# Second attention, stage boundaries, gates and low parts of a two-block transformer kernel: slabs, turns and copies in another order

## The reference, cut to what matters

```python
# first block, twice
h = rms_norm(x, norm_w)
q, k, v, z, q_h, f_h, i_h, g_h, gate_a, gate_h = split(h @ w_in)
a = window_attention(rope(q), rope(k), v, sinks) * silu(z)
b = rms(hgrn2(silu(q_h), f_h, i_h)) * silu(g_h)
x = x + (sigmoid(gate_a) * (a @ w_up_attn) + sigmoid(gate_h) * (b @ w_up_hgrn)) @ w_out
# second block, twice; the six vectors of mod come from silu(c) @ ada_w (48 slabs of 128 rows)
h = x * (1 + sc_t) + sh_t
y = mixer(h) @ w_o              # top-k attention, then differential attention
x = layer_norm(ALPHA * x + (1 + g_t) * y)
h = x * (1 + sc_c) + sh_c
x = layer_norm(ALPHA * x + (1 + g_c) * (square(relu(h @ w1)) @ w2))
```

## Time and profile before

| | us |
|---|---|
| median of 3 runs | 1178.76 |
| lowest, highest | 1177.69, 1179.79 |
| the profiled execution | 1179.56 |
| its span | 1177.8 |
| PE, POOL busy | 1080.7, 770.3 |
| ACT, DVE busy | 550.6, 507.2 |

### The profile page before, as it was taken

How to read it: one execution, slowest core, us unless ns; L and a number is a source line. 1 busy time by engine, 2 the same in 40 slices (tenths; PEclk the granted TensorE clock), 3 DMA queues, 4 the chain that set the end, 5 groups by cost and what they waited for, 6 DMA issues and landing times.

```text
span 1177.8 us, 16431 instructions
## 1 busy us (share of the span) xinstructions
PE 1080.7 (92%) x6638; PEld 910.6 (77%) x6638; DVE 507.2 (43%) x733; ACT 550.6 (47%) x769; POOL 770.3 (65%) x379
## 2 busy tenths in 40 slices
PE   5899989997899899899898999999999798999995
PEld 5877867886678687697577998897887378988984
DVE  5765433338555323465848101106725648110015
ACT  4654565455445654444543544444445334454441
POOL 5786665766665657573045887887875147888884
PEclk9999999998999999999999999999999799999998
DMA  7647733555375435663873868765667823755640
GB/s 242 207 125 277 230 110 116 160 174 162 97 275 196 130 105 145 223 223 108 303 250 110 300 219 281 252 216 161 211 211 240 304 90 111 222 187 181 194 144 36
DMA packets 112802, 221.63 MB, mean 188 GB/s; under 512 B 14945, under 2 KB 21463, under 8 KB 112727
## 3 DMA queue, kind: packets, MB, share of 16 engines
q1 hardware_dynamic: 107552, 210.30, 54.3%
q10 hardware_dynamic: 5174, 10.28, 2.5%
HBM read 219.48 MB, written 1.07 MB: 187 GB/s over the span
## 4 chain that ended last, share of the span: by engine, by line
PE 70%; DVE 12%; ACT 7%; POOL 6%; issue 4%; ACTq 1%; DMA 1%; DVEq 0%; SPq 0%; POOLq 0%
PE lin_ps L352 12%; PE lin_ps L353 11%; PE lin_ps L354 11%; PE tmp_ps L359 5%; POOL wlo L962 5%; PE tmp_ps L360 5%; PE tmp_ps L361 5%; PE lin_ps L359 3%; PE lin_ps L360 3%; PE lin_ps L361 3%; PE tmp_ps L612 3%; ACT whi L1071 2%; PE tmp_ps L511 2%; PE tmp_ps L414 1%; DVE qst L1464 1%
## 5 line engine op out<-in xcount | busy, mean ns | idle before, releaser
L962 POOL TENSOR_TENSOR wlo<-ring,whi 128x1024 fp32r<-128x1024 f32 (+2 forms) x304 | 733.4, 2424 | 337.3 <-ACT whi L1071 329.8
L1071 ACT CAST whi<-ring 128x1024 fp32r<-128x1024 f32 (+2 forms) x304 | 313.0, 1034 | 465.6 <-PE lin_ps L354 252.4
L352 PE MATMUL lin_ps<-whi,hThi 128*128 128x512 f32 (+2 forms) x528 | 209.7, 397 | 28.6 <-POOL wlo L962 14.5
L353 PE MATMUL lin_ps<-wlo,hThi 128*128 128x512 f32 (+2 forms) x528 | 204.3, 387 | 0.0
L354 PE MATMUL lin_ps<-whi,hTlo 128*128 128x512 f32 (+2 forms) x528 | 203.8, 386 | 0.0
L359 PE MATMUL tmp_ps<-hThi,whi 128*128 128x256 f32 x520 | 148.6, 286 | 6.0 <-DVEq L1756 5.5
L352 PEld LDWEIGHTS lin_ps<-whi,hThi 128*128 128x128 f32 x528 | 101.7, 193 | 61.7 <-issue 21.6
L360 PE MATMUL tmp_ps<-hTlo,whi 128*128 128x256 f32 x520 | 147.9, 284 | 0.0
L361 PE MATMUL tmp_ps<-hThi,wlo 128*128 128x256 f32 x520 | 147.8, 284 | 0.0
L1828 DVE TENSOR_TENSOR arena<-tmp_ps,arena 128x1024 f32<-128x1024 f32 x16 | 19.6, 1225 | 229.0 <-ACT arena L1286 228.9
L354 PEld LDWEIGHTS lin_ps<-whi,hTlo 128*128 128x128 f32 x528 | 101.6, 192 | 20.1
(11 more groups left out here) (273 smaller groups left out, 1496.7 us busy)
## 6 DMA issues: line engine op xcount, KB each, us to landing
ring<-in_mlp_w SPq DMA_DIRECT2D x128, 512.0 KB, 4.4
ring<-in_ada_w SPq DMA_DIRECT2D x82, 512.0 KB, 4.8
ring<-in_w_in SPq DMA_DIRECT2D x80, 512.0 KB, 5.4
ring<-in_b_w_in SPq DMA_DIRECT2D x24, 512.0 KB, 4.5
ring<-in_w_out SPq DMA_DIRECT2D x16, 512.0 KB, 3.4
arena<-in_ada_w SPq DMA_DIRECT2D x27, 256.0 KB, 5.1
ring<-in_a_w_in SPq DMA_DIRECT2D x12, 512.0 KB, 6.8
ring<-in_w_up_hgrn SPq DMA_DIRECT2D x8, 512.0 KB, 3.4
```

The lines of the kernel that those rows point to most:

```text
L352: pe.matmul(ps, xh, hi, start=first, stop=False, skip_group_check=True)
L353: pe.matmul(ps, xh, lo, start=False, stop=False, skip_group_check=True)
L962: pool.tensor_tensor(wlo[:, n % PARTS, :, 0:width], ring[:, u % RING, 2 * h:2 * h + 2, 0:width], whi[:, n % PARTS, :, 0:width].bitcast(F32 ...
L1071: act.copy(whi[:, n % PARTS, :, 0:width], ring[:, u % RING, 2 * h:2 * h + 2, 0:width]).then_inc(S("high_formed"), 1)
```

## The change

It is a bundle of edits to the order of work. Nothing that is computed changes.

1. **Second attention.** Before, 8 slabs stood in visits of 4, 2 and 2 after turns 4, 5 and 6. Now there are four visits of 2 after turns 6, 7, 8 and 9, and the first weights of w_o are reserved after turn 6. `ada_close` moves with the first visit. The DVE reads the visits after quads 6 and 7 and around `heads_scaled(0)`.
2. **Boundaries into s0 to s3.** `mixed` goes block by block instead of by pairs, over alternating banks (`BANKED`). One or both turns go to `lin_ps` (`TURNED_IN_LIN`). In s1 and s2 tile 0 is turned before the slabs. The filler of 4 stands behind the first product's opened PSUM; s3's filler goes from 16 to 12. `project` and the MLP's end finish column half 0 of y whole before the last products of half 1, and DVE's `residual` adds half 0 of both tiles first. `affine` is spread over the first MLP groups.
3. **Gates of f0 and f1.** ACT copies the gates and z raw; Silu and Sigmoid follow after the attention, in SBUF, on ACT. The turn of `a` moves from behind the `uh` products to between halves of the second.
4. **Low parts of f0 and f1.** POOL forms each `wlo` half in two instructions.
5. **End.** Tile 0's last scaling goes over ACT and POOL, tile 1's stays in PSUM until its last step on DVE; the four outputs wait on two semaphores.

```diff
+BANKED = (0, 2, 1, 3)
+TURNED_IN_LIN = {"s0": 1, "s1": 2, "s2": 1, "s3": 2}
+BUSY = {"f0": 14, "f1": 4, "s0": 4, "s1": 0, "s2": 0, "s3": 12}
...
+                if between and not early:
+                    between()
+                ps = opened_turn(0).rearrange("p a b -> p (a b)")
+                if early:
+                    tile(ps, 0)
+                    between()
+                else:
+                    keep_busy(ps[:, 0:HALF], BUSY[name])
+                    tile(ps, 0)
+                mm = tile(ps, 1)
+                closed_turn(mm, 0)
+                ps = opened_turn(1).rearrange("p a b -> p (a b)")
...
+                def turn_a():
+                    pe.wait_ge(S("f_a"), L + 1)
+                    feature_major(f"f{L}aT", hs[:, :, 0:HALF], 4)
...
-                    linear_tok(f"f{L}uh{c}", I["w_up_hgrn"][L], c * HALF, HALF, hT, kts=4, k_src=4)
-                pe.wait_ge(S("f_a"), L + 1)
-                feature_major(f"f{L}aT", hs[:, :, 0:HALF], 4)
+                    linear_part(f"f{L}uh{c}", I["w_up_hgrn"][L], c * HALF, HALF, hT, 0, kts=4, k_src=4,
+                                mid=turn_a if c else None)
...
-                part(0, 0)
-                output_turned(name, 1)
-                part(1, 0)
-                last_by_tiles(name, [opened[f"{name}y{c}"] for c in range(2)], w, 4, hT, 4)
+                linear_part(f"{name}y0", w, 0, HALF, hT, 0, half=turn_lin[f"{name}o0"][0],
+                            mid=lambda: output_turned(name, 1))
+                linear_part(f"{name}y0", w, 0, HALF, hT, 4)
+                opened[f"{name}y1"] = open_lin(f"{name}y1", turn_lin[f"{name}o1"][0])
+                last_by_tiles(name, w, [(1, 0, hT, 0, True, ()), (1, 4, hT, 4, False, ())])
...
-            mixed("s0", lambda: [reserve(*latent(k0)) for k0 in (0, 4)])
+            mixed("s0")
...
-                      after={4: lambda: (reserve(HALF, (slice(0, HALF), win(I["b_w_o_2"][0], 0, HALF, 0))), ada(4)),
-                             5: lambda: ada(2), 6: lambda: ada(2)})
+                      after={6: lambda: (reserve(HALF, (slice(0, HALF), win(I["b_w_o_2"][0], 0, HALF, 0))), ada(2)),
+                             7: lambda: ada(2), 8: lambda: ada(2), 9: lambda: ada(2)})
...
+                    cuts = (slice(0, 1), slice(1, 2)) if n < halves_at["f1y1"][0] else (slice(0, 2),)
+                    for cut in cuts:
+                        source = ring[:, u % RING, 2 * h:2 * h + 2, 0:width]
+                        ins = pool.tensor_tensor(wlo[:, n % PARTS, cut, 0:width], source[:, cut, :],
+                                                 whi[:, n % PARTS, cut, 0:width].bitcast(F32), ALU.subtract)
...
-                    read(act.activation(dst, ps, ACT.Sigmoid), name)
+                    read(act.copy(dst, ps), name)
...
+                act.wait_ge(*read_of(f"f{L}gh1"))
+                act.activation(zs[:], zs[:], ACT.Silu).then_inc(S("f_gates"), 1)
+                for c in range(2):
+                    cols = slice(c * HALF, (c + 1) * HALF)
+                    act.activation(gh[:, :, cols], gh[:, :, cols], ACT.Sigmoid).then_inc(S("f_gates"), 1)
+                high_parts(formed[0] + 1, halves_at[f"f{L}aT0"][1])
+                for c in range(2):
+                    cols = slice(c * HALF, (c + 1) * HALF)
+                    act.activation(ga[:, :, cols], ga[:, :, cols], ACT.Sigmoid).then_inc(S("f_gates"), 1)
...
+                        if k >= 2:
+
+                            act.wait_ge(S("mixed_low"), count.get("mixed_act", 0) + kk - 1)
...
+                dve.wait_ge(*done[f"{name}y0"])
+                summed(0, 0)
+                summed(1, 0)
+                dve.wait_ge(*done[f"{name}t1"])
+                summed(0, 1)
+                statistics(0)
```

303 lines of the change are left out of this document (178 added, 125 removed).

## The result

| | before | after |
|---|---|---|
| median | 1178.22 (4 runs) | 1152.54 (4 runs) |
| lowest, highest | 1176.97, 1179.79 | 1151.07, 1153.63 |
| ratio after to before | | 0.9781, 95% interval 0.9763 to 0.9798 |
| span of the profiled execution | 1177.8 | 1149.3 |

The forecast was 36.6 and 1142. Its wide range (1133 to 1157) holds the time, the narrow one (1137 to 1150) doesn't, and the time lies nearer to rival 1 (1156) than to the forecast. The two PE timelines, put side by side at the same instruction, tell where the 28.5 came from.

A forecast was written before the change was run, and what follows sets the result against it. PE, busy 92% of the span, was taken as the bound. Terms 7.3 + 11.9 + 8.6 + 5.8 + 3.0 = 36.6 off 1179.56 gave 1143.0, less 0.8 to the median 1142.2; range 1137 to 1150, wide 1133 to 1157.

The forecast's parts named there:

- rival 1: Gains overlap: half of the second attention's 7.3 and the boundaries' 11.9 goes, no clock comes back; 1156, chance 0.25.
- second attention with the output product: Second attention: scaling of the output starts 8.0 earlier, less a new wait of 0.7 in `project`; net 7.3.
- boundaries, s3 / s1 / s0 / s2: Into s0 to s3: first products start earlier once PE's waits for PSUM pairs fall away; 11.9 net of 0.8 at MLP ends.
- gates and low parts, f0 and f1: f0 and f1: ACT copies without table loads and moved turn of a, 8.6; POOL's low parts in two, 5.8.
- end: End of the program: tile 1's half 0 summed earlier, 3.3 less 0.3 for a lock; 3.0.
- Rival 2: More clock: all half-clock stretches after waits vanish, those in the attention and f1 too; 1134, chance 0.12.
- cast held in `mixed`: Boundaries: ACT, waiting in `mixed` for DVE's low parts, casts later; 1.5 in s0, 0.2 in s1.
- s1's and s3's MLP code is else untouched: Remark at the sum: the MLPs of s1 and s3 otherwise unchanged, so no further term.
- they land by 932 at most: Second attention, slabs of turns 8 and 9: slots free from 921.7, a megabyte in 2.7 us, landed by 932.
- 1.75 twice: PE's waits behind DVE adds blocked by whole POOL low parts (3.5 for L1610), part of the 5.8 low-parts term.
- Rival 3: Slower: DVE steps between the cut low parts and POOL's fixed part exceeds 0.17; 1241, chance 0.04.
- signs of being wrong: PE waits over 6 more on POOL in f0 and f1, on `ring<-in_ada_w` in turns 8 and 9, or on ACT in `uh`.

The follow-up runs named there:

- e1: Changed kernel with the second attention's slabs as before, in visits of 4, 2 and 2 after turns 4, 5 and 6; 1156.7 us.
- e8: Changed kernel with all turns of s0 to s3 in `tmp_ps` as before, block-by-block operand kept; 1170.6 us.
- e7: Changed kernel with the gates of f0 and f1 as before (Silu and Sigmoid while ACT empties PSUM), turn of a at its new place; 1156.9 us.
- e2: Changed kernel with POOL's low parts of f0 and f1 in one instruction each, as before; 1159.2 us.
- e3: Changed kernel with blocks 4 to 7 of each boundary by pairs in one bank, as before, so ACT waits for no low part in them; 1148.7 us.
- e12: Changed kernel with the 12 passes on x (layer norm's weight and bias) in s1, s2 and s3 left out; 1146.7 us.
- e5: Kernel of e3 with each pass on x of s1 and s3 moved behind the previous group's last hidden product; 1146.0 us.
- e4: Changed kernel with the four passes on x of s1 and s3 all behind the first product's operand, as before; 1163.1 us.
- e6: Changed kernel with the first of the second attention's four visits after turn 5 instead of 6; 1153.2 us.
- e9: Kernel of e5 with the second attention's fourth visit (2 slabs) moved behind the second output turn in the project; 1148.0 us.
- e11: Changed kernel with every low part cut in two, those of s0 to s3 too; 1160.6 us.
- e10: Kernel of e9 with the low parts of f0's first products whole, cut only from f0's level loop on; 1144.8 us.

## Why the prediction was right in the main and wrong by 10 us

| term | predicted | by the two traces | experiment |
|---|---|---|---|
| second attention with the output product | 7.3 | 4.8 (6.3 - 1.5) | e1: 3.6 for the visits (4.4 - 0.8) |
| boundaries, s3 / s1 / s0 / s2 | 4.0 / 4.6 / 2.8 / 1.2 | 3.9 / 4.2 / 1.9 / 1.1 | e8 |
| MLP ends | -0.8 | -1.1 | |
| gates and low parts, f0 and f1 | 8.6 + 5.8 | 16.1 | e7: 4.4 in the attention; e2: 6.7 |
| end | 3.0 | 3.2 | |
| first product of s2 | not foreseen | -2.4 | e3, e12 |
| first groups of s1, s3 | not foreseen | -1.5, -1.4 (0.4 - 1.9) | e5, e12 |
| output product of s0 | not foreseen | -0.3 | |
| sum | 36.6 | 28.5 | |

The turn of a, the MLPs' ends and the end of the program were not undone by themselves; their figures are differences of two traces, which is less than an experiment shows. Three slips stand in the prediction as well. Its heading gives 13.1 for the boundaries where its own terms add up to 12.6 and its sum takes 12.7 less 0.8. Rival 2 is put at 1134, where 1142 less 6 is 1136. And the fixed part of 0.17 does not come out of 1.86 and 2.40, which give 0.10; 0.15 was measured, so that figure was near by luck. What the prediction has the Trainium skill say of a stand (TensorE: Matmul & The Clock Gate, Part 1) is worked out from it: the page gives the dependence on phase for the warm-up alone. That a stand may or may not drop the clock is shown here by f0 and f1.

**Boundaries: right.** The first products of s1, s0 and s3 each start 2.03 after the first matmul of turn 1 (1.87 after the last one of turn 0 ends), and the clock reads 1.00 in the stretches that were at half. e8 shows that the pair of PSUM banks was the cause. The step that failed here is the cast held in `mixed`. In s0 it was priced at 1.5, and PE's wait is 1.84 there. For the others the text says "a cast held behind `mixed`'s new waits costs 0.2" for s1, and s2 stands at "near its whole wait". That sizing looked at one half. A late cast is a loss of lead, and what it costs is decided by what comes next to POOL. In s2 four passes on x come next, and 2.4 go.

**The passes on x: the step that failed most.** The sum says "s1's and s3's MLP code is else untouched". It was not: the diff spreads `affine` over the first groups, and the description of the change says so. It got no term. By the trace that I had, one could be made: in s2 a POOL operation takes 3.3 to 3.4 beside a pass (12.5 for the four passes, 836.38 to 848.92), where PE's pace is 2.88, so four of them without a lead cost PE about 2. A lone pass costs POOL 1.0, and PE up to 0.5. That gives 1 to 2 at each of three places, which is what came. e12 prices all of it at 5.8 (5.3 by the traces), e5 shows that most can be had back without leaving anything out, and e4 that without the spreading the bundle would have lost 10.6 more.

**Second attention: mechanism right, one term short.** DVE's chain is 8.3 shorter (8.0 forecast). The failed step is "they land by 932 at most". It took the bytes of four slabs alone, 10.8 from the first free slot on. In after that slot comes free as forecast: the first of the eight transfers of 512 KB is issued at 903.27, 18.4 before the 921.7 of the prediction. But it lands at 907.20, 3.9 later, where a following one takes 1.3, and two in the middle take 4.6 together (909.90 to 914.51), for a reason that the trace doesn't show. The last lands at 918.38, 4.8 later than my figure comes to on after's scale (932 less 18.4 is 913.6). w_o has no part in that: its transfers are issued from 912.05 on and land one by one behind, from 919.74 on. e6 shows that an earlier first visit doesn't help, e9 shows that behind the slabs w_o's own transfer is the next limit, through ACT's stream. The new wait of 0.7 in the output product was replaced by a stretch at half clock. Windows of after at its start:

```profile
924.00:926.00 2.00, 2.00 (x8) 1.56 (x7) 0.31 (x2) 0.00 (x0) 1.58 (x1) 0.62 1.06 388
926.00:928.00 2.00, 2.00 (x7) 1.57 (x6) 1.90 (x4) 0.00 (x0) 0.07 (x1) 0.52 1.01 371
```

The half takes 4.44 (924.01 to 928.45) instead of 2.72, so 1.7. PE had stood 1.02 before 922.96 and several times before that. It goes with the new place of the visits: e1 has no such stretch there. Which of the stands brings it isn't settled.

**Gates and low parts: near in sum, by places that differ.** Gates: the traces have 4.8 in f0 and 3.2 in f1 from the last level to the end, 8.0 in all against 8.6; e7 gives 4.4 of it to the copies (5.3 by its trace, 4.9 in the sum without the turn of a). Low parts: the other 8.1 of the 16.1 stand against 5.8, and not where I put them. The level loop of f0 gained 1.1, that of f1 4.4, and 2.5 came in the products ahead of f1's levels, where I had only a cost; there the wait for POOL of 4.08 and the half clock behind it are gone. The waits that I named, "1.75 twice", are still 1.43 and 1.65, and the one before the closing grew from 3.35 to 4.44. What went in the levels are 1.43 and 2.85 at L1619, now L1699, and with the latter the whole stretch at half clock behind it. I gave those to the low parts, and that is not shown: with whole low parts alone (e2) the 2.85 is 0.79, with the old gates alone (e7) it is 1.39, and neither has the half clock. So the match of e2's 6.7 with the 5.8 is in good part luck. PE of after in f1:

```profile
305.40 2.02 PE L646 MATMUL tmp_ps<-arena 128*128 128x128 f32 x16 [1.65 <-DVE arena L1690]
...
312.30 3.64 PE L545 MATMUL tmp_ps<-ring,csil 128*32 128x512 f32 x16 [4.44 <-DVE arena L1699]
```

POOL is busy all through that stretch (eight half operations in 12.19 from 297.11 on), and DVE's adds of 0.68 take 1.75 to 1.78 each: half the lock, met twice as often. My 1.3 of clock in f1 was low: 2.9 went there before, and all of it came back.

**End: right.** Last DVE step of after, against the earlier trace rows; it ends at 1146.4, 5.4 after PE where it was 9.1:

```profile
1145.03 1.41 DVE L1904 SCALAR_TENSOR_TENSOR x<-lin_ps,st,lnp 128x512 f32<-128x512 f32 x2
```

**Rivals.** Rival 1 gave nearly the time (1156), mostly for other reasons. It takes 3.7 from the second attention and 5.9 from the boundaries. The second attention lost 2.5 of its 7.3, in part by the DMA in turns 8 and 9 that the rival names, and the boundaries with the MLPs' ends 1.9 of 11.9. The clock, which it gave up, did come back at the boundaries. That the range holds the time is owed to that rival's bound and not to a term for what happened. Rival 2's condition nearly came true in the trace of after, which has two stretches at half clock left before its last matmul, and the time was 1152 all the same. Rival 3 (the cut low parts) does not act where it was put: in f0 and f1 the waits for POOL grew by 2.7, not by 6. But half of its mechanism is real: e11 shows DVE between the cuts at 8.1, with a fixed part no larger than 0.17. Of the signs of being wrong, one came: the waits on `ring<-in_ada_w` in turns 8 and 9, 2.8 in all. The rule of the Trainium skill (SBUF — State Buffer, section SBUF: two separate sides), whoever starts first holds the shared pair for a whole instruction, is borne out by e2 (an add of 0.68 takes 2.83) and e11 (a POOL operation of 1.30 takes 2.27). I applied it to f0 and f1 only, and it was in force at the three places that I missed.

## What to carry to other kernels

Price a late producer by what its consumer meets next, not by the delay: a lead of one half is worth nothing in one stage and 2.4 us in the next. When a diff moves work that holds something shared (here 1.2 us passes that block another engine), give each new place a term even if the work itself is off the path, and put such a pass where the blocked engine has a lead, or time to win it back. Cutting an operation shortens the other engine's wait and lengthens its own, so cut only where the other engine is what the bound engine waits for.

## What the runs showed of the hardware

- A DVE pass of two SBUF operands and a POOL operation take turns one by one when both have work queued. Four passes of 1.2 beside whole POOL operations take 13.05, beside half ones 8.58. Each pass costs POOL 1.0, whatever the size of its operation: 2.40 becomes 3.38 (after, s2), 1.30 becomes 2.25 to 2.28 (e11). From start to start a turn of both takes some 0.3 less than the two alone: 3.34 for 1.2 and 2.40, 2.2 for 1.2 and 1.30, 1.70 for 0.68 and 1.28 (after, f1). The DVE step queued behind the passes, which reads PSUM, is then late as well (e4: 7.14 on ACT).
- A POOL subtraction of 512 elements a partition is 1.30 undisturbed (2.55 for two, e11), 1024 elements 2.40: a fixed part of about 0.15, against the 0.17 worked out ahead.
- TensorE's clock fell to 0.50 after waits of 4.49 (e9) and 2.03 (e7, f0), stayed at 1.00 after another wait of 2.03 in the kernel before (f1), and near 498 in s0 it fell in three of the traces of the changed kernels and not in nine, with nothing changed at that place between after and e1 or between e9 and e10. A gain of 1 to 2 us behind one stand is no more than a chance.
- Transfers of 512 KB in one queue land one by one in the order of issue, 1.3 to 1.5 apart but for two at 2.5 and 2.1. One that finds the queue empty takes 3.6 to 3.9 (after, 886 to 926).
